# Three half feed-forwards of the second block by seven block products in place of eight, and a norm that squares tile by tile

## The chip, the cores and the metric

The kernel runs on one core of one Trainium2 chip, as one launch. The metric is the device time of that core in microseconds (us), the median over runs. The core has a matrix engine (TensorE, PE in the profile, with its weight loads as PEld), a vector engine (VectorE, DVE), a scalar engine (ScalarE, ACT), GpSimd (POOL) and SyncE (SP), which issues the weight transfers. Everything is float32. The runs of the kernel before: 3458.43, 3456.97 and 3460.97 us, median 3458.43.

## The reference

Two blocks of layers over 256 latent tokens with 1024 features; the second block also carries 256 context tokens. The change is in the second block, whose half feed-forward is:

```python
def swiglu(h, wg, wu, wd):
    return (jax.nn.silu(h @ wg) * (h @ wu)) @ wd

def half_ffn(h, g, shift, scale, gate, wg, wu, wd):
    return h + 0.5 * gate * swiglu(modulate(rms_norm(h, g), shift, scale), wg, wu, wd)

for l in range(DEPTH):          # DEPTH = 2; x: 256 latent tokens, ctx: 256 context tokens
    x   = half_ffn(x,   g_norm[l, 0], ml[0], ml[1], ml[2], ...)
    ctx = half_ffn(ctx, g_norm[l, 0], mc[0], mc[1], mc[2], ...)
    ... token mixing (attention, short convolution) on x and ctx ...
    x   = half_ffn(x,   g_norm[l, 2], ml[6], ml[7], ml[8], ...)
    if l < DEPTH - 1:
        ctx = half_ffn(ctx, g_norm[l, 2], mc[6], mc[7], mc[8], ...)
```

`wg` and `wu` are 1024 x 2816, `wd` is 2816 x 1024. `ml` and `mc` are modulation vectors of the latent and of the context tokens.

## The kernel before, in words

Activations are kept with features on the 128 partitions and tokens along the free axis. `x` is [128, 8 feature tiles, 512 tokens]: columns 0 to 255 are the context, 256 to 511 the latents. 2816 is 22 tiles of 128 (`FT`), 1024 is 8 (`KT`).

A half feed-forward (`HalfFfn`, run as half00, half01, half10 and half11, in that order, with the mixing stages mix0 behind half00 and mix1 behind half10) has three parts:

- the norm (`tensor_norm`, `scalar_norm`, `vector_norm`). ScalarE squares tiles 0, 2, 4, 6 (line 238) and VectorE tiles 1, 3, 5, 7 (line 224), each as its tile of `x` is ready; on VectorE the odd squares stand behind a wait for the last tile of `x` and the small scale operations (lines 1611, 1585). TensorE sums over partitions with a matrix of ones, eight matmuls in the order of the tiles, into `aux[0]`. ScalarE takes Ln and Exp (lines 241, 243) for the reciprocal root; VectorE scales (line 228) and ScalarE shifts (line 250), 16 half tiles each. The first group of matmuls behind it waits tile by tile, so it starts with the first shifted tile.
- the up part (`tensor_pairs`): 11 weight blocks of 2 MB, each with four groups (gate, up, gate, up) of 8 matmuls 128 x 128 by 128 x W. W is 512 in half00, half01 and half10, which carry context and latents, and 256 in half11. ScalarE takes Silu of the gate (line 1606), VectorE multiplies it with the up group into `big` (line 1618).
- the down part (`tensor_down`): 8 blocks of 1.4 MB, each with one group of 22 matmuls 128 x W. VectorE adds gate times result to `x` (line 1627).

PSUM has eight banks: `acc[0..3]` go round the groups, `aux[0..3]` serve the norms and the attention. A group waits until its bank was read (`acc_free`), and its last matmul raises `acc_full`. Weights go through four slots of 2 MB (`RING`, `SLOT`); SyncE issues block b once block b-4 is used up. `te.matmul` on float32 stands in the trace as two MATMUL records and two weight loads; all have line 130, since one helper (`mm`) issues them. The order on each engine is the order in which `tensor_program`, `scalar_program` and `vector_program` are written: each engine works its list in order and waits on semaphores. No planner changes it.

In the first block's recurrence (`scalar_scan`, `vector_scan`, four rounds) masks multiply 64 x 64 blocks, and one operand is copied with factor -1.

## Time and profile before

| | before |
|---|---|
| runs | 3458.43, 3456.97, 3460.97 us |
| profiled execution, its own time | 3464.32 us |
| span of the profile | 3463.0 us |
| mean granted TensorE clock | 0.986 |
| TensorE busy | 3323.2 us, 96% |
| VectorE busy | 751.0 us, 22% |
| ScalarE busy | 531.1 us, 15% |
| DMA, mean | 107 GB/s |
| half00, first matmul to last | 1236.9 to 1692.0 us |
| half01 | 2057.6 to 2514.0 us |
| half10 | 2525.4 to 2981.8 us |
| half11 | 3232.6 to 3461 us |

A start in the trace counts from the span's start. A row of the time order (timeline) gives start, length, engine, line, operation, output<-inputs, shapes and how many instructions were merged in it; in brackets the idle time of the engine before it and what ended it. The clock that a row of stretches (windows) gives is a share of full speed.

### The profile page before, as it was taken

Reading aid. Unit: us, or ns where it says so; the run is one execution under the profiler, and the core shown is the slowest. Engines: PE = TensorE matmul, PEld = TensorE weight load, DVE = VectorE, ACT = ScalarE, POOL = GpSimd, SP = SyncE. Lnnn points to the kernel's source line nnn. Section 1 sums busy time; section 2 is a strip of 40 time slices with the busy share of each in tenths; the row PEclk is TensorE's granted clock in tenths of the full one; section 3 lists DMA queues with packets and bytes.
Section 4 is the critical chain, followed back from the end, with each engine's and each line's share of the span. In section 5 each row is a group of like instructions: output and inputs, shape, how many; then the busy total and the mean of one; then the engine's idle time right before and its main releaser. Section 6 shows DMA issues by size and latency. Waiting matters only on the chain.

```text
span 3463.0 us, 33245 instructions
## 1 busy us (share of the span) xinstructions
PE 3323.2 (96%) x14466; PEld 2023.5 (58%) x14466; DVE 751.0 (22%) x1670; ACT 531.1 (15%) x1114; POOL 50.5 (1%) x78
## 2 busy tenths in 40 slices
PE   7889999998899999999999999999999999999999
PEld 5656678885688844444443644444444444555888
DVE  3255333123432110000115510000010000235100
ACT  1133222022221110000113310000010000223100
POOL 0000000020000000000001000000000000000000
PEclk9899999999999999999999999999999999999999
DMA  5359934463044522213203012222322222220343
GB/s 209 114 198 324 334 129 149 140 182 125 29 145 133 160 86 84 65 50 91 73 21 97 1 49 73 73 60 76 95 73 73 65 67 74 75 92 25 123 144 99
DMA packets 355813, 370.23 MB, mean 107 GB/s; under 512 B 7395, under 2 KB 282228, under 8 KB 355540
## 3 DMA queue, kind: packets, MB, share of 16 engines
q1 hardware_dynamic: 350224, 358.04, 32.6%
q0 software_dynamic: 2224, 5.38, 0.8%
q10 hardware_dynamic: 3220, 4.68, 0.4%
q8 instruction: 115, 1.88, 0.2%
q14 instruction: 30, 0.25, 0.0%
HBM read 367.03 MB, written 1.05 MB: 106 GB/s over the span
## 4 chain that ended last, share of the span: by engine, by line
PE 93%; DVE 4%; ACT 3%; issue 1%; DMA 0%; ACTq 0%; DVEq 0%
PE acc L130 82%; PE aux L130 10%; ACT sb_work L1486 0%; DVE sb_big L1333 0%; ACT sb_work L1350 0%; ACT sb_work L1352 0%; DVE sb_work L1538 0%; DVE sb_work L1554 0%; DVE sb_work L1535 0%; DVE sb_xn L228 0%; DMA sb_x<-xT 0%; DVE sb_work L1523 0%; ACT sb_rstd L241 0%; ACT sb_rstd L243 0%; ACT sb_xn L250 0%
## 5 line engine op out<-in xcount | busy, mean ns | idle before, releaser
L130 PE MATMUL acc<-sb_xn,weights 128*128 128x256 f32 (+1 forms) x5888 | 1842.9, 475 | 29.5 <-ACT sb_xn L250 17.1
L130 PEld LDWEIGHTS acc<-sb_xn,weights 128*128 128x128 f32 x5888 | 1120.4, 191 | 743.9 <-issue 645.0
L130 PE MATMUL acc<-sb_big,weights 128*128 128x256 f32 (+1 forms) x2304 | 727.0, 478 | 0.0
L130 PEld LDWEIGHTS acc<-sb_big,weights 128*128 128x128 f32 x2304 | 439.1, 191 | 286.2 <-issue 253.3
L1618 DVE TENSOR_TENSOR sb_big<-sb_work,acc 128x512 f32<-128x512 f32 (+1 forms) x88 | 54.6, 621 | 998.3 <-PE acc L130 998.3
L130 PE MATMUL aux<-sb_work 128*128 128x128 f32 (+8 forms) x1206 | 190.9, 340 | 35.5 <-DVE sb_work L1544 9.7
L1606 ACT ACTIVATE sb_work<-acc 128x512 f32<-128x512 f32 (+1 forms) x88 | 47.9, 544 | 973.1 <-PE acc L130 973.1
L130 PEld LDWEIGHTS aux<-sb_work 128*128 128x128 f32 (+4 forms) x1206 | 130.6, 180 | 113.7 <-issue 54.0
L1627 DVE SCALAR_TENSOR_TENSOR sb_x<-acc,sb_small,sb_x 128x256 f32<-128x256 f32 x56 | 24.9, 479 | 504.9 <-PE acc L130 504.9
L130 PE MATMUL acc<-sb_work,weights 128*128 128x256 f32 (+4 forms) x312 | 102.4, 467 | 6.1 <-DVE sb_work L1122 6.0
L238 ACT ACTIVATE sb_xn<-sb_x 128x256 f32<-128x256 f32 (+1 forms) x40 | 18.4, 496 | 471.4 <-DVE sb_x L1627 412.4
L130 PE MATMUL acc<-weights,sb_work 128*32 128x512 f32 (+1 forms) x608 | 88.9, 598 | 1.2 <-issue 1.2
L130 PE MATMUL aux<-sb_xn,sb_ones 128*128 128x256 f32 (+1 forms) x180 | 62.9, 496 | 23.6 <-ACT sb_xn L238 17.7
L1214 DVE SCALAR_TENSOR_TENSOR sb_work<-acc,sb_cols,sb_work 128x255 f32<-128x255 f32 x88 | 42.5, 482 | 195.0 <-ACT sb_work L1202 195.0
L130 PEld LDWEIGHTS acc<-sb_work,weights 128*128 128x128 f32 (+2 forms) x312 | 54.7, 179 | 46.4 <-issue 39.4
L1202 ACT ACTIVATE sb_work<-acc,sb_cols 128x256 f32<-128x256 f32 x88 | 49.7, 564 | 191.4 <-PE acc L130 191.4
L130 PEld LDWEIGHTS aux<-sb_xn,sb_ones 128*128 128x128 f32 x180 | 34.5, 199 | 49.0 <-issue 27.7
L130 PE MATMUL acc<-sb_big 64*128 64x512 f32 (+3 forms) x144 | 56.7, 528 | 1.8 <-DVE sb_work L1913 1.0
L272 DVE TENSOR_TENSOR sb_x<-acc,sb_x 128x256 f32<-128x256 f32 x32 | 13.6, 425 | 196.5 <-PE acc L130 196.5
L1359 POOL TENSOR_TENSOR sb_big<-sb_big,sb_rope 96x256 f32<-96x256 f32 (+1 forms) x32 | 23.2, 724 | 2174.0 <-PE aux L130 2174.0
L1851 ACT ACTIVATE sb_work<-acc,sb_work 128x512 f32<-128x512 f32 (+1 forms) x72 | 43.9, 614 | 43.4 <-DVE sb_work L1924 42.3
L1922 DVE TENSOR_REDUCE sb_work<-acc 128x1 f32<-128x512 f32 (+1 forms) x60 | 41.5, 691 | 28.9 <-PE acc L130 28.9
(260 smaller groups left out, 1583.2 us busy)
## 6 DMA issues: line engine op xcount, KB each, us to landing
weights<-ffn_w_up SPq DMA_DIRECT2D x88, 1024.0 KB, 7.9
weights<-w_mod SPq DMA_DIRECT2D x36, 2048.0 KB, 9.1
weights<-ffn_w_down SPq DMA_DIRECT2D x48, 1408.0 KB, 7.0
weights<-ffn_w_gate SPq DMA_DIRECT2D x44, 1024.0 KB, 5.5
weights<-w_in SPq DMA_DIRECT2D x8, 2048.0 KB, 8.1
weights<-mix_w_in SPq DMA_DIRECT2D x6, 2048.0 KB, 13.4
weights<-na_w_qkv SPq DMA_DIRECT2D x6, 2048.0 KB, 8.0
weights<-ple_w_gate SPq DMA_DIRECT2D x4, 2048.0 KB, 8.6
```

The lines of the kernel that those rows point to most:

```text
L130: return te.matmul(o, lhsT, rhs, start=start, stop=stop, skip_group_check=True)
L238: square_a.on(ac.activation(N.squares[:, k, :], x[:, k, N.t0:T2], ACT.Square))
L272: acc_free[g.bank].on(ve.tensor_tensor(x[:, k, t0:t1], acc[g.bank][:, 0:t1 - t0], x[:, k, t0:t1], ALU.add))
L1202: mid_tap.on(ac.activation(u, acc[g.bank][:, 0:L], ACT.Identity, scale=cols("ffn_cw", 1, 132 * F.i + 44 + t), bias=cols("ffn_cb", 1, 44 * ...
L1214: v_step.on(ve.scalar_tensor_tensor(u[:, 1:L], ps[:, 0:L - 1], cols("ffn_cw", 1, 132 * F.i + t), u[:, 1:L], ALU.mult, ALU.add))
L1359: hn_cos.on(gp.tensor_tensor(raw[:, CTX:], raw[:, CTX:], rot[1], ALU.mult))
L1606: acc_free[g.bank].on(ac.activation(F.sg[:, f % 2, :], acc[g.bank][:, 0:F.W], ACT.Silu))
L1618: acc_free[u.bank].on(ve.tensor_tensor(F.hid[:, f, :], F.sg[:, f % 2, :], acc[u.bank][:, 0:F.W], ALU.mult))
L1627: ve.scalar_tensor_tensor(x[:, k, a:e], acc[g.bank][:, a - t0:e - t0], gate_of(k, h), x[:, k, a:e], ALU.mult, ALU.add))
L1851: ins_ = ac.activation(mx_e[:, b, W * i:W * i + W], acc[b][:, W * i:W * i + W], ACT.Exp, bias=mx_st[:, 6 + 2 * b + i:7 + 2 * b + i], scale ...
L1922: v_step.on(ve.tensor_reduce(top, src, AX.X, ALU.max))
```

## The change

Two adjacent operands are treated as 2 x 2 blocks, and their product is made by the Strassen-Winograd scheme: seven block products in place of eight, with sums of blocks before and behind them.

Up part: block rows are gate and up weights of one 128-wide tile of the hidden dimension, the inner halves are feature tiles 0 to 3 and 4 to 7, and block columns are context and latents. So one step i (of 22) makes seven products of 4 matmuls 128 x 256, where two groups of 8 matmuls 128 x 512 stood. Down part: block rows are two neighbouring output tiles, the inner halves are hidden tiles 0 to 10 and 11 to 21; each of 4 steps makes seven products of 11 matmuls 128 x 256 in place of two groups of 22 matmuls 128 x 512. The order of the products is `PRODUCTS` = 1, 3, 2, 6, 7, 5, 4. Product 1 goes to bank A, is copied out by ScalarE, and product 2 is accumulated on it; products 7 and 4 share bank C in the same way, with VectorE reading in between.

VectorE makes the sums: four of the weights per step (`weight_sums`; 512 elements per partition in the up part, 1408 in the down part, one of them in place in the weight slot), four of the activations per part (`activation_sums`; 1024 and 2816 elements), and behind the products five sums of 256 elements that read PSUM. `weight_sums(0)` stands ahead of the norm on VectorE. Product 1 of step 0 waits for all tiles of the norm.

The norms of mix0, half10 and mix1 (`hooked`) are squared by ScalarE alone, two tiles behind each down step, into two buffers, and TensorE's eight matmuls of the norm stand in the down part of the feed-forward before (six behind product 2 of a step, two at its end). The norms of half00 and half01 keep the old form. half11 is unchanged.

In the recurrence of the first block a mask that held -upto and before holds upto and before for both uses, so that it is loaded once; the factor -1 moves from one copy of ScalarE to another and to one of VectorE. Some scratch areas have other addresses.

The diff, cut to its core:

```diff
+    def stream(loads=1):
+        return Block(b % RING, weights_in[b % RING].reserve(loads)(loads - 1), reuse, [])
...
     def tensor_norm(N):
-        W = T2 - N.t0
-        for k in range(KT):
-            te.wait_ge((square_a, square_v)[k % 2].sem, N.sq[1 - k % 2](k // 2))
-            ins_ = mm(aux[0][:, 0:W], ones[:], N.squares[:, k, :], k == 0, k == KT - 1)
-        sq_total.on(ins_)
+        for k in range(KT) if not N.hooked else ():
+            tensor_norm_tile(N, k)
+
+    def scalar_square(N, k):
+
+        ac.wait_ge(N.x_ready[k][0].sem, N.x_ready[k][1])
+        if k >= 2:
+            ac.wait_ge(sq_total.sem, N.total(k - 2))
+        square_a.on(ac.activation(N.squares[:, k % 2, :], x[:, k, N.t0:T2], ACT.Square))
...
-    sil, pick = area(work, 12128, KT, 32), area(work, 12384, 2)
-    side = area(work, 12400, 2, 128)
+    sil, pick = area(work, 12416, KT, 32), area(work, 12672, 2)
+    side = rope[:, 2, 384:512]
...
-        sc_tm.on(ac.activation(by_b, quads(aux[0][:]), ACT.Copy, scale=-1.0))
+        sc_tm.on(ac.copy(by_b, quads(aux[0][:])))
...
-        sc_uwa.on(ac.copy(uw[:, 4:8, :], quads(b1[:])))
+        sc_uwa.on(ac.activation(uw[:, 4:8, :], quads(b1[:]), ACT.Copy, scale=-1.0))
...
-        sc_uwv.on(ve.tensor_copy(uw[:, 0:4, :], quads(b0[:])))
+        sc_uwv.on(ve.tensor_scalar(uw[:, 0:4, :], quads(b0[:]), -1.0, None, ALU.mult))
...
+    PRODUCTS = (1, 3, 2, 6, 7, 5, 4)
+    hook_sq = area(xn, FH * L, 2, T2)
+    bank_a, bank_b, bank_c, bank_d, bank_e = acc[0], acc[1], acc[2], acc[3], aux[0]
...
+            self.norm = Norm(0, xv_w, lambda k, h: gsc[:, k, h:h + 1], x_ready, lambda k, h: mod[:, m0 + k, h:h + 1],
+                             extra, squares, hooked)
+            self.up = [stream(loads=2) for _ in range(FH)]
+            self.down = [stream() for _ in range(KT)]
+            self.last_up = last_done[-KT - 1]
...
+    def tensor_fast(F, following):
+        tensor_norm(F.norm)
+        for i in range(F.n):
...
+            for blk in F.blocks_of(i):
+                te.wait_ge(weights_in[blk.slot].sem, blk.arrived_at)
+            a11, a12, s3, a22 = F.weights(i)
+            s1, s2, s4 = F.sums(i)
+            t1, t2, t4 = sum_x if up else sum_h
+            src, kt = (xv_w, 4) if up else (hid, FH)
+            b11, t3, b21, b22 = src[:, 0:kt, 0:L], src[:, 0:kt, L:T2], src[:, kt:2 * kt, 0:L], src[:, kt:2 * kt, L:T2]
+            operands = {1: (a11, b11), 2: (a12, b21), 3: (s4, b22), 4: (a22, t4), 5: (s1, t1), 6: (s2, t2), 7: (s3, t3)}
+            banks = {1: bank_a, 2: bank_a, 3: bank_e, 4: bank_c, 5: bank_d, 6: bank_b, 7: bank_c}
+            for q in PRODUCTS:
+                if q == 1 and i and i <= FT:
+                    te.wait_ge(st_g1.sem, F.g1(i - 1))
+                elif q == 1 and i:
+                    te.wait_ge(st_x.sem, F.x(4 * (i - FT - 1)))
+                elif q == 3:
+                    te.wait_ge(st_s.sem, F.s(i))
+                    if i:
+                        te.wait_ge(st_c12.sem, F.c12(i - 1))
+                    if i == FT:
+                        te.wait_ge(st_hid.sem, F.hid(2 * FT - 1))
+                elif q == 2:
+                    te.wait_ge(st_u.sem, F.u(i))
+                elif q == 7 and i:
+                    te.wait_ge(st_c21.sem, F.c21(i - 1))
+                elif q == 4:
+                    te.wait_ge(st_v.sem, F.v(i))
+                if i in (0, FT) and q in (6, 7, 5, 4):
+                lhs, rhs = operands[q]
+                for k in range(kt):
+                    if i == 0 and q == 1 and k == 0:
+                        sig, value = F.norm.ready(KT - 1)
+                        te.wait_ge(sig.sem, value)
+                    if i == FT and q == 1:
+                        te.wait_ge(st_hid.sem, F.hid(2 * k + 1))
+                    ins_ = mm(banks[q][:, 0:L], lhs[:, k, :], rhs[:, k, :], k == 0 and q not in (2, 4), k == kt - 1)
+                F.done[i, q][0].on(ins_)
+                if q == 2 and i > FT:
+                    for k in (2 * (i - FT) - 2, 2 * (i - FT) - 1):
+                        tensor_norm_tile(following, k)
+        for k in (KT - 2, KT - 1):
+            tensor_norm_tile(following, k)
...
+        for i in range(F.n):
+            s = i % 2
+            ac.wait_ge(F.done[i, 1][0].sem, F.done[i, 1][1])
+            if i >= 2 and i - 2 < FT:
+                ac.wait_ge(st_hid.sem, F.hid(2 * (i - 2) + 1))
+            elif i >= 2:
+                ac.wait_ge(st_x.sem, F.x(4 * (i - 2 - FT) + 3))
+            st_u.on(ac.copy(pair_u[:, s, :], bank_a[:, 0:L]))
+            if i < FT:
+                ac.wait_ge(F.done[i, 2][0].sem, F.done[i, 2][1])
+                st_g1.on(ac.activation(pair_g1[:, s, :], bank_a[:, 0:L], ACT.Silu))
+                ac.wait_ge(st_c12.sem, F.c12(i))
+                st_g2.on(ac.activation(pair_g2[:, s, :], pair_g2[:, s, :], ACT.Silu))
+            elif i > FT:
+                scalar_square(following, 2 * (i - FT) - 2)
+                scalar_square(following, 2 * (i - FT) - 1)
+        scalar_square(following, KT - 2)
+        scalar_square(following, KT - 1)
+
+    def vector_fast(F):
+        hid = area(big, 0, FT, T2)
+        sig, value = F.norm.x_ready[KT - 1]
+
+        def weight_sums(i):
+            a11, a12, a21, a22 = F.weights(i)
+            s1, s2, s4 = F.sums(i)
+            for blk in F.blocks_of(i):
+                ve.wait_ge(weights_in[blk.slot].sem, blk.arrived_at)
+            if 2 <= i < FT:
+                ve.wait_ge(F.done[i - 2, 5][0].sem, F.done[i - 2, 5][1])
+            elif i > FT:
+                ve.wait_ge(F.done[i - 1, 5][0].sem, F.done[i - 1, 5][1])
+            v_step.on(ve.tensor_tensor(s1, a21, a22, ALU.add))
+            ve.wait_ge(v_step.sem, v_step.n)
+            v_step.on(ve.tensor_tensor(s2, s1, a11, ALU.subtract))
+            v_step.on(ve.tensor_tensor(a21, a11, a21, ALU.subtract))
+            ve.wait_ge(v_step.sem, v_step.n)
+            st_s.on(ve.tensor_tensor(s4, a12, s2, ALU.subtract))
...
+        def activation_sums(src, kt, t):
+            st_t.on(ve.tensor_tensor(t1, b12, b11, ALU.subtract))
+            ve.wait_ge(st_t.sem, st_t.n)
+            st_t.on(ve.tensor_tensor(t2, b22, t1, ALU.subtract))
+            st_t.on(ve.tensor_tensor(b12, b22, b12, ALU.subtract))
+            ve.wait_ge(st_t.sem, st_t.n)
+            st_t.on(ve.tensor_tensor(t4, b21, t2, ALU.subtract))
+
+        ve.wait_ge(sig.sem, value)
+        weight_sums(0)
+        v_step.on(ve.tensor_scalar(half_gate, mod[:, F.m0 + 16:F.m0 + 24, :], 0.5, None, ALU.mult))
+        vector_scales(F.l, 0 if F.j == 0 else 2, F.m0 + 8)
+        vector_norm(F.norm)
+        sig, value = F.norm.ready(KT - 1)
+        ve.wait_ge(sig.sem, value)
+        activation_sums(xv_w, 4, sum_x)
+        for i in range(F.n):
+            s, down = i % 2, i - FT
+            u, v, g1, g2 = (t[:, s, :] for t in (pair_u, pair_v, pair_g1, pair_g2))
+            if i < FT:
+                weight_sums(i + 1)
+            elif down == 0:
...
+            if down >= 0:
+                ve.wait_ge(F.done[i, 2][0].sem, F.done[i, 2][1])
+                add_back(2 * down, 0, bank_a[:, 0:L])
+            ve.wait_ge(st_u.sem, F.u(i))
+            ve.wait_ge(F.done[i, 6][0].sem, F.done[i, 6][1])
+            v_step.on(ve.tensor_tensor(u, u, bank_b[:, 0:L], ALU.add))
+            ve.wait_ge(v_step.sem, v_step.n)
+            ve.wait_ge(F.done[i, 7][0].sem, F.done[i, 7][1])
+            st_v.on(ve.tensor_tensor(v, u, bank_c[:, 0:L], ALU.add))
+            ve.wait_ge(F.done[i, 5][0].sem, F.done[i, 5][1])
+            v_step.on(ve.tensor_tensor(g2, u, bank_d[:, 0:L], ALU.add))
+            ve.wait_ge(st_v.sem, st_v.n)
+            v_step.on(ve.tensor_tensor(v, v, bank_d[:, 0:L], ALU.add))
+            ve.wait_ge(v_step.sem, v_step.n)
+            st_c12.on(ve.tensor_tensor(g2, g2, bank_e[:, 0:L], ALU.add))
+            if down >= 0:
+                ve.wait_ge(st_c12.sem, st_c12.n)
+                add_back(2 * down, 1, g2)
+                add_back(2 * down + 1, 1, v)
+                if i + 1 < F.n:
+                    weight_sums(i + 1)
+            ve.wait_ge(F.done[i, 4][0].sem, F.done[i, 4][1])
+            st_c21.on(ve.tensor_tensor(u, u, bank_c[:, 0:L], ALU.add))
+            ve.wait_ge(st_c21.sem, st_c21.n)
+            if i < FT:
+                ve.wait_ge(st_g2.sem, F.g2(i))
+                st_hid.on(ve.tensor_tensor(hid[:, i, L:T2], g2, v, ALU.mult))
+                ve.wait_ge(st_g1.sem, F.g1(i))
+                st_hid.on(ve.tensor_tensor(hid[:, i, 0:L], g1, u, ALU.mult))
+            else:
+                add_back(2 * down + 1, 0, u)
...
-    half00 = HalfFfn(0, 0, 0, ple1.x_ready, extra=(ctx_in, 32))
-    mix0 = Mixing(0, True, half00.x_ready)
-    half01 = HalfFfn(0, 1, 0, mix0.x_ready)
-    half10 = HalfFfn(1, 0, 0, half01.x_ready)
-    mix1 = Mixing(1, False, half10.x_ready)
+    half00 = FastFfn(0, 0, ple1.x_ready, extra=(ctx_in, 32))
+    mix0 = Mixing(0, True, half00.x_ready, hooked=True)
+    half01 = FastFfn(0, 1, mix0.x_ready, squares=area(big, 0, KT, T2))
+    half10 = FastFfn(1, 0, half01.x_ready, squares=hook_sq, hooked=True)
+    mix1 = Mixing(1, False, half10.x_ready, hooked=True)
```

## Rows read from the trace of the kernel before

**Rows 1.** The page, part 1 (busy time and share of span) and part 4 (chain that ended last).

```profile
PE 3323.2 (96%) x14466; PEld 2023.5 (58%) x14466; DVE 751.0 (22%) x1670; ACT 531.1 (15%) x1114; POOL 50.5 (1%) x78
...
PE 93%; DVE 4%; ACT 3%; issue 1%; DMA 0%; ACTq 0%; DVEq 0%
```

**Rows 2.** Time order, ScalarE: Silu of the gate in half00, steps 2 and 22.

```profile
1259.47 0.60 ACT L1606 ACTIVATE sb_work<-acc 128x512 f32<-128x512 f32 x1 [13.14 <-PE acc L130]
...
1534.14 0.60 ACT L1606 ACTIVATE sb_work<-acc 128x512 f32<-128x512 f32 x1 [13.14 <-PE acc L130]
```

**Rows 3.** Time order where matmuls are 128 x 256: ffn0's groups of 8, half11's of 22.

```profile
601.56 0.56 ACT L1202 ACTIVATE sb_work<-acc,sb_cols 128x256 f32<-128x256 f32 x1 [1.40 <-PE acc L130]
...
629.19 0.56 ACT L1202 ACTIVATE sb_work<-acc,sb_cols 128x256 f32<-128x256 f32 x1 [1.41 <-PE acc L130]
...
3394.29 0.48 DVE L1627 SCALAR_TENSOR_TENSOR sb_x<-acc,sb_small,sb_x 128x256 f32<-128x256 f32 x1 [9.08 <-PE acc L130]
...
3460.77 0.48 DVE L1627 SCALAR_TENSOR_TENSOR sb_x<-acc,sb_small,sb_x 128x256 f32<-128x256 f32 x1 [9.02 <-PE acc L130]
```

**Rows 4.** Stretch of ffn0: length, PE, PEld, DVE, ACT, POOL busy, clock, DMA.

```profile
600.00:640.00 40.00, 40.00 (x188) 35.20 (x187) 11.24 (x24) 6.90 (x14) 0.00 (x0) 1.00 0.42 110
```

**Rows 5.** Time order at the start of half00.

```profile
1226.02 0.42 DVE L1275 TENSOR_TENSOR sb_x<-sb_work,sb_x 128x256 f32<-128x256 f32 x1
...
1226.89 2.50 DVE L224 TENSOR_TENSOR sb_xn<-sb_x 128x512 f32<-128x512 f32 x4
...
1227.64 6.28 PE L130 MATMUL aux<-sb_xn,sb_ones 128*128 128x512 f32 x14 [0.42 <-DVE sb_xn L224]
...
1235.85 6.50 ACT L250 ACTIVATE sb_xn<-sb_xn,sb_mod 128x256 f32<-128x256 f32 x16 [0.55 <-DVE sb_xn L228]
1236.90 10.52 PE L130 MATMUL acc<-sb_xn,weights 128*128 128x512 f32 x20 [2.99 <-ACT sb_xn L250]
...
1245.74 0.60 ACT L1606 ACTIVATE sb_work<-acc 128x512 f32<-128x512 f32 x1 [2.09 <-PE acc L130]
```

**Rows 6.** Stretches at the same place: the granted clock.

```profile
1239.00:1241.00 2.00, 2.00 (x4) 0.89 (x3) 2.00 (x6) 2.00 (x6) 0.00 (x0) 0.50 0.00 0
1241.00:1243.00 2.00, 2.00 (x6) 0.79 (x5) 0.76 (x2) 1.98 (x5) 0.00 (x0) 0.99 0.00 0
```

**Rows 7.** Time order from half00 into mix0.

```profile
1673.19 0.88 DVE L1627 SCALAR_TENSOR_TENSOR sb_x<-acc,sb_small,sb_x 128x256 f32<-128x256 f32 x2 [18.01 <-PE acc L130]
1674.10 0.63 ACT L238 ACTIVATE sb_xn<-sb_x 128x512 f32<-128x512 f32 x1 [37.14 <-DVE sb_x L1627]
1674.75 1.28 ACT L239 ACT_TABLE_LOAD   x1
...
1692.08 0.88 DVE L1627 SCALAR_TENSOR_TENSOR sb_x<-acc,sb_small,sb_x 128x256 f32<-128x256 f32 x2 [18.01 <-PE acc L130]
...
1693.81 6.28 PE L130 MATMUL aux<-sb_xn,sb_ones 128*128 128x512 f32 x14 [0.92 <-DVE sb_xn L224]
1700.12 0.69 ACT L241 ACTIVATE sb_rstd<-aux,sb_small 128x512 f32<-128x512 f32 x1 [24.09 <-PE aux L130]
...
1703.08 9.25 PE L130 MATMUL acc<-sb_xn,weights 128*128 128x512 f32 x21 [2.99 <-ACT sb_xn L250]
```

**Rows 8.** Time order at the start of half01, TensorE and ScalarE.

```profile
2057.61 17.84 PE L130 MATMUL acc<-sb_xn,weights 128*128 128x512 f32 x34 [2.99 <-ACT sb_xn L250]
...
2067.76 0.60 ACT L1606 ACTIVATE sb_work<-acc 128x512 f32<-128x512 f32 x1 [3.40 <-PE acc L130]
```

**Rows 9.** Time order from half01 into half10, VectorE and TensorE.

```profile
2514.09 0.87 DVE L1627 SCALAR_TENSOR_TENSOR sb_x<-acc,sb_small,sb_x 128x256 f32<-128x256 f32 x2 [18.01 <-PE acc L130]
...
2525.43 5.46 PE L130 MATMUL acc<-sb_xn,weights 128*128 128x512 f32 x6 [2.99 <-ACT sb_xn L250]
```

**Rows 10.** Groups by line and shape: VectorE sums from SBUF, 1024 and 256 elements.

```profile
L474 DVE TENSOR_TENSOR sb_work<-sb_work 128x1024 f32<-128x1024 f32 x1 | 1.2, 1224 | 0.0
...
L1220 DVE TENSOR_TENSOR sb_big<-sb_work 128x256 f32<-128x256 f32 x44 | 18.7, 425 | 1.5
```

More of the change, by code:

```diff
@@ L2007, in tensor_program @@
         tensor_ple(ple1)
[L2008 removed]
+        tensor_fast(half00, mix0.norm)
         tensor_mixing(mix0)
[L2010 to L2011 removed]
+        tensor_fast(half01, half10.norm)
+        tensor_fast(half10, mix1.norm)
         tensor_mixing(mix1)
```

120 lines of the change are left out of this document (95 added, 25 removed).

## The prediction

> **What bounds the kernel now.** I read the page's busy times and its chain first, then the spacing of results in the two kinds of feed-forward, then the gaps between stages. TensorE is busy 96% of the span and carries 93% of the chain that ended last [rows 1]. So a half feed-forward is as long as its matmuls, plus the gap around its norm. The reader is to see how even the results come: from step 2 to step 22 of half00 the Silu starts 274.67 us apart over 20 steps, 13.73 us for 16 matmuls of 512 columns, or 0.8583 us each [rows 2]. The down part has the same pace: 18.89 us for 22 [rows 7]. Where a matmul has 256 columns, eight groups of 8 take 27.63 us in ffn0, 0.4317 us each, and seven groups of 22 take 66.48 us in half11, 0.4317 us each [rows 3]. Two things follow. A matmul of half the width costs 0.503 of the wide one, so the shorter products lose next to nothing. And a group of 8 has the same pace as a group of 22, so the change of bank and the waits that are already satisfied at a group's end cost some nanoseconds at most. ffn0 keeps that pace, with TensorE busy 40.00 of 40 us at full clock, while VectorE works 11.24 us of them [rows 4]. The rest of the time around a feed-forward is the norm: a gap of 11.0 us from half00's last matmul to mix0's first [rows 7].
>
> **The matmuls.** Before, each of the three feed-forwards has 44 x 8 + 8 x 22 = 528 matmuls of 0.8583 us, 453.2 us. After, it has 22 x 7 x 4 + 4 x 7 x 11 = 924 of 0.4317 us, 398.9 us. Saved: 54.3 us each, 162.9 us in all. A product is 4 or 11 matmuls long, shorter than any group in the rows. There are 26 x 7 = 182 handovers in each feed-forward, 546 in all. From groups of 8 and 22 I take them at nothing. If every one made TensorE really wait, the nearest row is a matmul that starts when a VectorE square ends: the first square takes some 0.69 us from 1226.89 and the matmul starts at 1227.64, 0.06 us later [rows 5]. That gives 33 us as the upper bound. I take 1 us, as the rows with satisfied waits are the nearest: **161.9 us saved**.
>
> **Does anything reach TensorE late inside a step?** Up part: a product is 4 x 0.4317 = 1.73 us, a step 12.09 us. Product 2 waits for ScalarE's copy of product 1 (256 elements; the Silu of 512 takes 0.60 us [rows 2]), and product 3 stands in between with 1.73 us. Even a table load of 1.28 us [rows 7] before that copy would end within 0.2 us of that. VectorE has per step four weight sums of 512 elements (the four squares of 512 took 2.50 us [rows 5]; two waits for its own results add some 0.1 us each, 2.7 us) and eight sums of 256 at 0.48 us or less [rows 3], so some 6.7 of 12.09 us. The tightest point is product 6: behind product 4 of the step before, VectorE has three of the small sums (1.5 us), then the weight sums, until 4.2 us; product 6 ends at 4 x 1.73 = 6.9 us. Nothing waits.
>
> Down part: a step is 33.2 us. The weight sums of the next step share one buffer, so they stand between the end of product 5 and the start of the next product 3: products 4 and 1, 22 x 0.4317 = 9.50 us. In this window VectorE has five operations of 256 (5 x 0.51 = 2.55 us) and four sums of 1408 elements. No row has that size; 256 elements take 0.425 and 1024 take 1.224 us [rows 10], so 1.04 ns per element more, 1.62 us at 1408, and with two of the four overlapping slightly 6.5 us. Together 9.05 us: a slack of only 0.45 us. I take no stall. Each 0.1 us by which a sum is longer costs nothing up to the slack and then 0.4 us at each of 9 places. The activation sums of the down part (2816 elements, 3.1 us each) begin some 1.5 us into products 1, 3, 2 (14.2 us); product 6 needs only two of them, 7.7 us. The loads keep four slots and the same 2 MB per 24.2 us in place of 27.5; the DMA share in ffn0, which takes 2 MB in 13.8 us, is 0.42 [rows 3, 4].
>
> For a sum of 1408 elements the Trainium skill (VectorE: DVE Perf Modes, The TRN2 errata) gives (N + 151) / 0.96 ns, which would be 1.62 us as an estimate. No run here shows this size yet; the sum would be the same.
>
> **The entries of half00 and half01** get longer in two ways. First, `weight_sums(0)` stands on VectorE ahead of the odd squares, and behind it queue the scales and the squares, for which TensorE waits: 2.7 us. Nothing covers it. Second, product 1 waits for the last shifted tile. Before, the first matmul started at 1236.90, 1.05 us behind the first shift, and the last shift ended at 1235.85 + 6.50 = 1242.35 [rows 5]; the matmuls in between ran beside the norm. After, the start moves 5.45 us later. Together 8.15 us each, **16.3 us lost**. What the slow clock costs I leave as it is: half00's first group took 8.84 us in place of 6.87 [rows 5], with a clock of 0.50 of full speed (1.2 GHz) after a gap of 2.99 us, and full speed from 1241 on [rows 6]; half01's took 10.15 us [rows 8]. These starts already pay 2.0 and 3.3 us, and a longer gap can hardly make them pay much more.
>
> **The hooked norms** (mix0, half10, mix1). Six of their eight matmuls of 512 now stand among the products: 6 x 0.858 = 5.15 us each, **15.4 us lost**; the seventh runs while VectorE adds the last tile. The gap shrinks. After the last product: two operations of VectorE 1.05, square 0.63 [rows 7], table load 1.28 (longer than the last norm matmul, 0.86), then, as before, from Ln to the first matmul 1703.08 - 1700.12 = 2.96 us [rows 7], with handovers 6.0 us. Before it was 1703.08 - 1692.08 = 11.0 us. So mix0 and mix1 gain 5.0 us each, **10 us won**, and with their six matmuls come out even. half10 gains the same 5.0, but its product 1 waits 5.45 us more for the last shift. The result is 11.4 us against 2525.43 - 2514.09 = 11.34 [rows 9]: nothing. `weight_sums(0)` is covered there: it ends at 1.05 + 2.7 = 3.75 us, and the reciprocal root is set at 4.4; without that cover it would cost 2.7 us.
>
> The Trainium skill (TensorE: Matmul & The Clock Gate, HAM oscillation) has a rule that speaks against this change: gaps in which TensorE idles throw it back to half clock, and each longer gap at an entry (8.5 us here) risks a restart at half speed. The trace agrees that such a gap can do it; as all three starts are already slow in places, the sum would be up to 3 us worse for each by it.
>
> **The rest.** In the recurrence, one mask load becomes smaller and a factor moves between copies of the same size in four rounds. half11 and the first block's norms get an extra signal per matmul. No row separates these; I take 0, bounds -1 to +1 us.
>
> **Sum.** 161.9 - 16.3 - 15.4 + 10 - 0 = 140.2 us. On the profiled execution 3464.3 - 140.2 = 3324.1; the runs' median lies 5.9 us below that execution, so **3318 us**.
>
> **Rivals.** (a) Handovers cost: each product waits some 0.06 us for something, 546 x 0.06 = 33 us, 3351. For it: twice to three times as many waits per matmul as in any group shown, and products of 1.73 us. Against: groups of 8 and 22 at one pace. (b) The slack of 0.45 us in the down part isn't there, because sums of 1408 elements read weight slots beside transfers and weight loads and take, say, twice as long: 4 x 1.62 - 0.45 = 6.0 us late at 9 places, 54 us, 3372. In the up part the doubled sums would end at 6.9 us, just in time. For it: no row has such a sum. Against: VectorE's 28% beside TensorE in ffn0 shows no slowing. (c) Slower than before: the clock. If short waits between products, not only gaps at the norm, make it fall to 1.2 GHz, a feed-forward takes up to twice its 398.9 us. The gain of 140 us is gone once 280 of the 1197 us of matmuls run at half clock, and at 350 us the kernel stands at 3493. Against: the small gaps between groups in ffn0 leave the clock at 1.00 [rows 4]. (d) The change doesn't do what it says, in that the norm in the down part isn't even: if the gap at mix0, half10 and mix1 stays at 11 us because another wait is last, 15 us, 3333.
>
> **Chances.** Forecast 0.70 (own range 3306 to 3326: clock at the starts -6 to +6, handovers, recurrence), (d) 0.08, (a) 0.11, (b) 0.08, (c) 0.03. The range takes in the forecast, (d) and half of (a): 3305 to 3343. A measurement of this kernel tells 0.2%, some 7 us, from no change. Only (c) lies there or beyond: faster 0.97, same 0.01, slower 0.02.
>
> **What would show it.** Right: product spacing of 1.73 us, up steps of 12.09, down steps of 33.2 plus 1.72 where two norm matmuls stand; TensorE idle only at the entries, 8.5 us from the last norm matmul to product 1; 6 us from half00's last product to mix0's first matmul. Wrong: a group of idle times of TensorE ahead of product 3 released by VectorE's weight sums (b), idle time or a pace above 0.432 us spread over all products (a), a granted clock below 1.00 inside the steps (c).

## The result, and the profile after

The changed kernel takes 3326.43 us (median; 3324.26 to 3327.29) against 3459.02 us of the kernel before in the same comparison: ratio 0.9616, 95% interval 0.9599 to 0.9632. That is 132.6 us less. The prediction was 3318 us, 140.2 us of gain in the profiled execution. The profiled executions stand 138.5 us apart (3464.32 and 3325.86). So the sum of the prediction is 1.7 us off, with an error of 4.5 us inside it that other differences partly cancel, and most of the 8 us by which the median misses comes from elsewhere. The median lies inside the range of 3305 to 3343 us, and just above the narrower one of 3306 to 3326 that the forecast gave for itself. One later execution of the changed kernel took 4228.42 us at a mean granted clock of 0.744, unlike all others; its cause is open, and it is left out of every median here.

The page of the kernel after, parts 1 and 4 (to be read against [rows 1]):

```profile
PE 3161.3 (95%) x16842; PEld 2474.9 (74%) x16842; DVE 1237.0 (37%) x2528; ACT 579.4 (17%) x1270; POOL 50.3 (2%) x78
...
PE 91%; DVE 4%; ACT 3%; issue 1%; DMA 1%; ACTq 0%; DVEq 0%
```

TensorE works 161.9 us less, VectorE 486 us more, and the kernel is still bound by TensorE. VectorE's share of the chain stays at 4%, in spite of its 486 us of new work. The stretch of half00's up part shows why (columns: length, then busy time of PE, PEld, DVE, ACT, POOL, granted clock, DMA share, GB/s):

```profile
1260.00:1500.00 240.00, 240.00 (x1114) 211.27 (x1113) 114.52 (x237) 23.09 (x60) 0.00 (x0) 1.00 0.26 80
```

TensorE never idles in 240 us and VectorE is busy 114.52 of them. The copy of each product 1 (time order of the kernel after, ScalarE: start, length, what; in brackets the idle time before) has a period of 12.09 us, seven products of 1.73 us, all through the up part of each of the three feed-forwards:

```profile
1261.86 0.37 ACT L1776 COPY sb_work<-acc 128x256 f32<-128x256 f32 x1 [1.80 <-PE acc L130]
...
1273.94 0.37 ACT L1776 COPY sb_work<-acc 128x256 f32<-128x256 f32 x1 [1.80 <-PE acc L130]
...
1286.03 0.37 ACT L1776 COPY sb_work<-acc 128x256 f32<-128x256 f32 x1 [1.79 <-PE acc L130]
```

In the down part, around the tightest place, time order of VectorE and TensorE:

```profile
1544.48 1.62 DVE L1801 TENSOR_TENSOR sb_work<-weights 128x1408 f32<-128x1408 f32 x1
...
1549.33 1.62 DVE L1806 TENSOR_TENSOR sb_work<-weights,sb_work 128x1408 f32<-128x1408 f32 x1
...
1551.74 4.91 PE L130 MATMUL aux<-sb_big,sb_work 128*128 128x256 f32 x22
```

A sum of 1408 elements takes 1.62 us, as estimated, beside transfers that move 290 GB/s from 1544 to 1552 us. The last one ends at 1550.95 and product 3, which reads it, starts at 1551.74 without idle time: a slack of 0.79 us where 0.45 us was predicted.

The entry of half00 is where the prediction was off ([rows 5] before). Time order of the kernel after:

```profile
1225.26 0.69 DVE L1801 TENSOR_TENSOR sb_work<-weights 128x512 f32<-128x512 f32 x1
...
1228.34 2.50 DVE L237 TENSOR_TENSOR sb_xn<-sb_x 128x512 f32<-128x512 f32 x4
...
1229.09 7.97 PE L130 MATMUL aux<-sb_xn,sb_ones 128*128 128x512 f32 x14 [3.08 <-DVE sb_xn L237]
...
1239.00 6.49 ACT L263 ACTIVATE sb_xn<-sb_xn,sb_mod 128x256 f32<-128x256 f32 x16 [0.55 <-DVE sb_xn L241]
...
1245.63 3.75 PE L130 MATMUL acc<-sb_xn,weights 128*128 128x256 f32 x8 [8.58 <-ACT sb_xn L263]
1249.18 2.28 PE L130 MATMUL aux<-sb_xn,sb_work 128*128 128x256 f32 x8
1251.30 1.89 PE L130 MATMUL acc<-sb_xn,weights 128*128 128x256 f32 x8
1253.02 1.89 PE L130 MATMUL acc<-sb_work 128*128 128x256 f32 x8
```

The weight sums hold the squares back (idle time 3.08 us in place of 0.42), and product 1 waits for the last shift (8.58 in place of 2.99). The third thing was not in the sum: the seven norm matmuls take 7.97 us in place of 6.28. The granted clock of the kernel after (same columns as above) shows it at half speed there:

```profile
1229.00:1233.00 4.00, 3.92 (x5) 1.63 (x6) 1.84 (x4) 0.00 (x0) 0.00 (x0) 0.57 0.68 216
1233.00:1237.00 4.00, 4.00 (x10) 1.52 (x8) 0.00 (x0) 0.00 (x0) 0.00 (x0) 1.00 0.00 0
```

In the first 4 us TensorE runs at a mean clock of 0.57, mostly at 1.2 GHz, and starts 5 of the trace's matmul records, against 10 in the next 4 us at 2.4 GHz. At the start of half01 it is the same, with 3.91 us of idle time (1.26 before) and 8.85 us:

```profile
2005.17 2.50 DVE L237 TENSOR_TENSOR sb_big<-sb_x 128x512 f32<-128x512 f32 x4
2005.92 8.85 PE L130 MATMUL aux<-sb_big,sb_ones 128*128 128x512 f32 x14 [3.91 <-DVE sb_big L237]
...
2023.34 3.75 PE L130 MATMUL acc<-sb_xn,weights 128*128 128x256 f32 x8 [8.57 <-ACT sb_xn L263]
```

From half00 into mix0, where the hooked norm was to pay ([rows 7] before; last product to first matmul 11.0 us), time order of the kernel after:

```profile
1652.05 0.42 DVE L1861 TENSOR_TENSOR sb_work<-sb_work,acc 128x256 f32<-128x256 f32 x1 [2.62 <-PE acc L130]
...
1653.03 0.63 ACT L279 ACTIVATE sb_xn<-sb_x 128x512 f32<-128x512 f32 x1 [3.33 <-DVE sb_x L1837]
1653.68 1.28 ACT L252 ACT_TABLE_LOAD   x1
...
1657.99 10.43 PE L130 MATMUL acc<-sb_xn,weights 128*128 128x512 f32 x18 [3.16 <-ACT sb_xn L263]
```

From 1652.01 (the last product's end, just ahead of L1861) to 1657.99 there are 5.98 us: 6.0 were predicted.

### The profile page after: what moved, and what is told of

Same layout as the page of the kernel before. It is cut to its first block, busy times and chain, and to the rows that moved or that the text cites. A ratio compares the mean times of both kernels' runs of the same rounds, so it can differ in the third digit from the quotient of the medians.

```text
span 3324.6 us, 39320 instructions
## 1 busy us (share of the span) xinstructions
PE 3161.3 (95%) x16842; PEld 2474.9 (74%) x16842; DVE 1237.0 (37%) x2528; ACT 579.4 (17%) x1270; POOL 50.3 (2%) x78
## 4 chain that ended last, share of the span: by engine, by line
PE 91%; DVE 4%; ACT 3%; issue 1%; DMA 1%; ACTq 0%; DVEq 0%
PE acc L130 75%; PE aux L130 16%; ACT sb_xn L263 1%; ACT sb_work L1508 0%; DVE sb_big L1355 0%; ACT sb_work L1372 0%; DMA weights<-mix_w_in 0%; ACT sb_work L1374 0%; DVE sb_work L1560 0%; DVE sb_work L1576 0%; DVE sb_work L1557 0%; DMA sb_x<-xT 0%; DVE sb_work L1545 0%; ACT sb_rstd L254 0%; ACT sb_rstd L256 0%
## 5 line engine op out<-in xcount | busy, mean ns | idle before, releaser
L130 PE MATMUL acc<-sb_xn,weights 128*128 128x256 f32 (+1 forms) x5360 | 1310.5, 400 | 47.7 <-ACT sb_xn L263 34.4
L130 PEld LDWEIGHTS acc<-sb_xn,weights 128*128 128x128 f32 x5360 | 1020.6, 191 | 298.3 <-issue 161.0
L130 PE MATMUL acc<-sb_big,weights 128*128 128x256 f32 x2040 | 448.3, 379 | 0.0
L130 PE MATMUL acc<-sb_work 128*128 128x256 f32 x1320 | 308.4, 379 | 0.0
L130 PE MATMUL acc<-sb_work,weights 128*128 128x256 f32 (+4 forms) x1104 | 285.7, 404 | 6.1 <-DVE sb_work L1144 6.0
L130 PEld LDWEIGHTS acc<-sb_work 128*128 128x128 f32 x1320 | 250.8, 190 | 37.9 <-issue 4.3
L130 PEld LDWEIGHTS acc<-sb_work,weights 128*128 128x128 f32 (+2 forms) x1104 | 205.1, 187 | 66.9 <-issue 39.4
L1844 DVE TENSOR_TENSOR sb_work<-sb_work,acc 128x256 f32<-128x256 f32 x78 | 32.9, 421 | 259.2 <-PE acc L130 259.2
L130 PE MATMUL aux<-sb_xn,sb_work 128*128 128x256 f32 x528 | 125.8, 381 | 0.0
L130 PEld LDWEIGHTS aux<-sb_xn,sb_work 128*128 128x128 f32 x528 | 101.4, 192 | 14.2
L1847 DVE TENSOR_TENSOR sb_work<-sb_work,acc 128x256 f32<-128x256 f32 x78 | 32.9, 422 | 137.1 <-PE acc L130 137.1
L1849 DVE TENSOR_TENSOR sb_work<-sb_work,acc 128x256 f32<-128x256 f32 x78 | 32.9, 421 | 131.9 <-PE acc L130 131.9
```

The lines of the kernel that those rows point to most:

```text
L130: return te.matmul(o, lhsT, rhs, start=start, stop=stop, skip_group_check=True)
L1844: v_step.on(ve.tensor_tensor(u, u, bank_b[:, 0:L], ALU.add))
L1847: st_v.on(ve.tensor_tensor(v, u, bank_c[:, 0:L], ALU.add))
L1849: v_step.on(ve.tensor_tensor(g2, u, bank_d[:, 0:L], ALU.add))
```

## The experiments

"Entry" below is the time from the end of the last addition to x to the first matmul of product 1. What a stage "takes" is counted from its first matmul to the end of its last addition to x, so a stage and the entry of the next one together make the whole. All ratios are against the kernel before, all diffs against the kernel after. Where a run is said to be some us less than after, it is against 3326.43 us.

**The kernel after once more**, so that the later runs have a neighbour.

> The changed kernel once more, beside the next three on the same chip. Both theories: 3326 us, and entries of half00 and half01 of 20 to 22 us from the last tile of x to product 1, of which the clock at half speed takes a part that differs by some us from run to run.

3324.7 us, ratio 0.9612 (0.9599 to 0.9625); with these four executions the median of all eight of the kernel after is still 3326.43. Entries 20.4, 21.3 and 10.6 us, as in the first profile. What is read from the entries repeats to 0.1 us.

**The weight sums behind the squares.** VectorE squares first, then prepares step 0.

```diff
+        if behind_squares is not None:
+            behind_squares()
         ve.wait_ge(rstd_set.sem, N.rstd)
...
-        weight_sums(0)
...
-        vector_norm(F.norm)
+        vector_norm(F.norm, lambda: weight_sums(0))
```

> The first weight sums move from ahead of the norm's odd squares to behind them on VectorE, nothing else. My theory: in half00 and half01 the sums (2.7 us) stretched TensorE's idle time before the second norm matmul to 3 to 4 us, and the norm matmuls behind it then ran at half clock for a while (7.97 and 8.85 us where seven took 6.28 before). With the sums away both go: 2.7 us twice, and 1.7 and 2.6 us of slow clock, 9.7 us in all, 3317 us; the seven norm matmuls take 6.3 us again. Rival: they were slow because of the weight transfers that run at that moment; then only 5.4 us are won, 3321 us, and they still take 8 to 9 us.

3323.12 us, 0.9610 (0.9596 to 0.9623). Time order of this kernel, TensorE, at both entries:

```profile
1229.32 6.28 PE L130 MATMUL aux<-sb_xn,sb_ones 128*128 128x512 f32 x14 [0.42 <-DVE sb_xn L237]
...
2002.78 6.28 PE L130 MATMUL aux<-sb_big,sb_ones 128*128 128x512 f32 x14 [1.26 <-DVE sb_big L237]
```

Without the long idle time the seven matmuls are back at 6.28 us. The entries fall by 4.4 and 5.2 us to 16.0 each, 9.6 us in all (theory: 9.7, of which only 5.4 are the sums themselves). Over all runs it is the same: in the six profiled kernels and repeats that leave the sums in front and the gap empty the seven take 7.8 to 8.0 us in half00 and 7.7 to 8.9 in half01, and in the six whose idle time there is 0.4 and 1.3 us they take 6.28 each time. A transfer into the weights runs beside these matmuls in both kernels, here even a denser one, at full clock:

```profile
1229.32:1233.00 3.68, 3.68 (x9) 1.77 (x10) 3.65 (x6) 1.26 (x1) 0.00 (x0) 1.00 1.09 371
```

So the transfer isn't what slowed them. But the median fell by only 3 us, to near the rival's 3321 and not for its reason: mix1 took 238.1 us in place of 234.4, half10 1.4 us more and half11 1.7.

**The same again**, since that remainder was unexplained.

> The weight sums behind the squares once more. In its first profile the entries of half00 and half01 got 4.3 and 5.2 us shorter, 9.5 in all, but the median only 4 us (3323 against 3327), because the mixing stage mix1 and half11 took 5.3 us longer than in the changed kernel, with a slow clock inside mix1. Theory: that is chance (where the slow clock falls in the attention of mix1), and a second set of runs lies anywhere from 3316 to 3324 us, with the entries again 9.5 us shorter. Rival: the earlier start itself costs the time later, so that the median stays at 3323 us and mix1 and half11 are longer again by 5 us.

3322.66 us, 0.9608 (0.9595 to 0.9621). Entries 16.0 us each again, and mix1 238.1 and half11 230.4 again: the numbers are those of the rival, not of the theory of chance. Where mix1's time goes is one stretch of its attention. Twenty microseconds of it in this kernel, and the same place in the kernel before:

```profile
2984.30:3004.30 20.00, 20.00 (x75) 11.10 (x75) 8.93 (x26) 6.80 (x16) 0.00 (x0) 0.77 0.06 19
```

```profile
3132.80:3152.80 20.00, 20.00 (x96) 11.90 (x95) 11.59 (x32) 8.28 (x20) 0.00 (x0) 1.00 0.08 24
```

TensorE counts as busy all through in both, but at a clock of 0.77 the trace holds 75 matmul records in place of 96. Ahead of it, in both kernels, stands a stretch in which TensorE is busy 15.38 of 20 us (2964.3 to 2984.3 and 3112.8 to 3132.8).

**The kernel before once more**, to see whether an unchanged kernel does this too.

> The kernel before once more. Its profiled execution took 3464.3 us against 3459 for the median of its runs. If that distance is chance (how much of the entries falls on half clock), this profile lies at 3457 to 3462 us; if profiling makes this kernel longer by 5 us, it lies at 3464 again.

3460.18 us, 0.9997 (0.9988 to 1.0005), but its profiled execution took 3472.54 us, outside both expectations. Its mix1 took 237.8 us in place of 233.4, with the same dip:

```profile
3135.00:3155.00 20.00, 20.00 (x76) 11.11 (x76) 9.02 (x26) 6.79 (x16) 0.00 (x0) 0.78 0.05 15
```

Its first block took 4.7 us more, half11 1.7 more, half10 3 less. half10's start shows that the same wait goes either way: 2.99 us of idle time behind the same matmuls, and then, in the first profile and in this one (granted clock 0.51 and 1.00, 8 and 14 matmul records):

```profile
2525.43:2531.43 6.00, 6.00 (x8) 2.51 (x9) 4.85 (x13) 5.98 (x15) 0.00 (x0) 0.51 0.01 3
```

```profile
2530.48:2536.48 6.00, 6.00 (x14) 2.73 (x15) 4.86 (x13) 5.98 (x15) 0.00 (x0) 1.00 0.01 3
```

So one execution of one kernel may or may not fall to half clock in these places, at 3 to 5 us each. A profile alone can't be trusted to better than that. The dip (mix1 at 237.8 to 238.8 us) is there in this run, in both kernels with the sums moved, with tile by tile, with both edits and with eight products, and absent (234.4 to 234.6) in the other seven profiles of the changed kernel and its variants. So no single edit decides it. Nor does the stage's time alone: mix1 starts at 2844.27 us in the repeat with the sums moved and dips, and at 2844.39 in the kernel with filled gaps and doesn't. The kernel after and the one with the sums moved each showed the same state in both of their profiles, the kernel before showed both states; what sets it stays open.

**Product by product, tile by tile.** Products 1, 3 and 2 of step 0 wait for each shifted tile as they read it.

```diff
-                    if i == 0 and q == 1 and k == 0:
-                        sig, value = F.norm.ready(KT - 1)
+                    if i == 0 and q in (1, 3, 2):
+                        sig, value = F.norm.ready(k if q == 1 else kt + k)
```

> Products 1, 3 and 2 of step 0 wait for the norm tile by tile, as the first group did in the kernel before; nothing else. My theory: product 1 starts some 5.4 us earlier, products 1 and 3 run beside the shifts, and product 6 starts 3.0 us earlier at full clock, up to 5.0 us where the slow clock after the gap now falls into time that waits for tiles anyway: 9 to 15 us over three entries, 3311 to 3317 us. Rival: the slow clock only moves with the start, so that nothing beyond 1 to 2 us each is won: 3320 to 3323 us.

3316.83 us, 0.9589 (0.9576 to 0.9602): 10 us less than after. The entries are 14.7, 15.8 and 5.0, each 5.5 to 5.7 us shorter. The feed-forwards take 408.7 us each in place of 407.4, 407.6 and 406.7, since some of the wait is now between the products. The second term of the entries was a real wait, and most of it can be had back (12 of 17 us).

**Both edits.**

> Both edits: weight sums behind the squares, and step 0 tile by tile. My theory: the two add up, 3326 - 9.7 - 12 = 3304 us (3300 to 3309). Rival: they take from the same slow clock, and together give no more than the larger of the two, 3314 us.

3308.32 us, 0.9564 (0.9551 to 0.9577), 18 us less than after: entries 10.5, 10.5 and 4.9. In the entries the gains of the two edits add up (9.9 us in half00, from 4.4 and 5.7); the median is 4 us above the theory, and mix1 takes 238.8 us here. Time order of this kernel, TensorE, at half00:

```profile
1224.35 6.28 PE L130 MATMUL aux<-sb_xn,sb_ones 128*128 128x512 f32 x14 [0.42 <-DVE sb_xn L237]
1233.61 3.60 PE L130 MATMUL acc<-sb_xn,weights 128*128 128x256 f32 x8 [2.99 <-ACT sb_xn L265]
```

**The norm at the end.** The eight squares and norm matmuls stand behind the last product in place of between the products.

```diff
-                if q == 2 and i > FT:
-                    for k in (2 * (i - FT) - 2, 2 * (i - FT) - 1):
-                        tensor_norm_tile(following, k)
-        for k in (KT - 2, KT - 1):
+        for k in range(KT):
             tensor_norm_tile(following, k)
```

(ScalarE's squares likewise.)

> The squares and the eight norm matmuls of mix0, half10 and mix1 all stand at the end of the feed-forward before, as one piece, with the same two buffers; the products are unchanged. My theory (interleaving moves 5.15 us into the steps and takes as much off the gap): the steps get 5.15 us shorter, the gap from the last product to the next stage's first matmul grows from 6.0 to some 10 us, so 3326 - 15.4 + 12.6 = 3323 us, 3320 to 3327. Rival: interleaving was a real gain, the norm's matmuls among the products cost nothing there; then 12 to 15 us slower, 3338 to 3341 us.

3324.92 us, 0.9607 (0.9592 to 0.9623). Time order of this kernel, TensorE, from half00 into mix0:

```profile
1642.91 4.91 PE L130 MATMUL acc<-sb_work,weights 128*128 128x256 f32 x22
1647.66 7.60 PE L130 MATMUL aux<-sb_xn,sb_ones 128*128 128x512 f32 x16
1658.41 7.11 PE L130 MATMUL acc<-sb_xn,weights 128*128 128x512 f32 x16 [3.15 <-ACT sb_xn L263]
```

The feed-forwards take 402.3, 402.4 and 401.7 us in place of 407.4, 407.6 and 406.7 (5.0 to 5.2 less each; six matmuls of 0.858 are 5.15), and the entries behind them are 9.6, 15.5 and 9.9 us in place of 5.0, 10.6 and 5.0 (4.6 to 4.9 more). The norm among the products is even, as the sum had it: the matmuls cost TensorE nearly the same in either place. Besides, mix0 takes 341.6 us here in place of 344.1: its first 8 us run at a granted clock of 1.00, against 0.57 in the kernel after. Whether the eight matmuls right ahead of the gap do that, or chance, one profile doesn't tell.

**Eight products.** Product 5 is computed twice, so that TensorE has eight block products and all else stays. The result isn't changed by it.

```diff
+                if q == 5:
+                    for k in range(kt):
+                        ins_ = mm(banks[q][:, 0:L], lhs[:, k, :], rhs[:, k, :], k == 0, k == kt - 1)
```

> Product 5 is computed twice, so that each step has eight products of the same size in place of seven. My theory (TensorE's matmuls alone set the pace, 0.4317 us each, and handovers cost nothing): 132 matmuls more in each of three feed-forwards, 57.0 us each, 171 us, 3497 us, 1.1% slower than the kernel before. Rival (VectorE or the handovers have a share in the pace of a step): part of the eighth product is hidden, 3440 to 3480 us.

3503.33 us, 1.0116 (1.0098 to 1.0134): 44 us slower than before, with all of the additions and none of the saving. The feed-forwards take 464.4, 464.0 and 464.0 us, 57.1, 56.4 and 57.2 more, where 132 matmuls of 0.4317 us make 57.0. The steps are one product longer to the hundredth:

```profile
1264.18 0.37 ACT L1779 COPY sb_work<-acc 128x256 f32<-128x256 f32 x1 [1.80 <-PE acc L130]
...
1277.99 0.37 ACT L1779 COPY sb_work<-acc 128x256 f32<-128x256 f32 x1 [1.80 <-PE acc L130]
```

13.81 us are 8 x 1.727. Only the number of matmuls sets the pace. The 6 us by which the median lies above the theory of 3497 are in mix0 and mix1, which took 3.4 and 3.6 us more than after; the added products don't explain that, and a dip of the clock as above would.

**One sum more in the down part.** One weight sum of 1408 elements is made twice with the same result.

```diff
             v_step.on(ve.tensor_tensor(s2, s1, a11, ALU.subtract))
+            if i > FT:
+                ve.wait_ge(v_step.sem, v_step.n)
+                v_step.on(ve.tensor_tensor(s2, s1, a11, ALU.subtract))
```

> In the down part one of the four weight sums of 1408 elements is made twice in the last three of four steps. My theory: in the trace of the changed kernel the sums end 0.79 us before product 3 starts, and one sum more costs 1.65 us, so product 3 waits 0.86 us in 9 steps: 7.7 us, 3334 us, and TensorE shows 9 idle times of 0.9 us ahead of product 3. Rival: VectorE has more room than that, because product 3 waits for something else: no change, 3326 us.

3336.38 us, 0.9638 (0.9623 to 0.9653). What TensorE waits for in this kernel between 1500 and 1660 us (us in total, times, longest):

```profile
PE aux L130 <- DVE sb_work L1809: 2.3, 3, 0.8
```

The same view of the kernel after, from 1240 to 1640 us, holds no wait of a product for VectorE, only the entry:

```profile
PE acc L130 <- ACT sb_xn L263: 8.6, 1, 8.6
```

1.65 us more of VectorE make TensorE idle for 0.8 us, so there is a slack of some 0.8 us, three times in each feed-forward. They get 3.2 to 3.3 us longer, which is more than 3 x 0.8. From one product's start to the next the trace shows the rest: product 3 starts 5.68 us behind product 1 in place of 4.75, and the product behind it 4.85 us later in place of 4.74. That is 1.03 us per step; in an unbroken row product 3 starts at 1551.74, before the record of the product ahead of it ends (1551.90), and behind a wait it doesn't.

**The idle gaps filled.** TensorE runs matmuls of 256 columns, which nobody reads, while it would wait: 6 behind the first norm matmul, 18 ahead of product 1.

```diff
+    def busy(n):
+        for _ in range(n):
+            mm(aux[2][:, 0:L], ones[:], rope[:, 0, 0:L])
...
+            if k == 0:
+                busy(fill)
...
+        tensor_norm(F.norm, 6)
+        busy(18)
```

> The changed kernel, with matmuls that nobody reads (128 x 256, into a bank that is free here) in TensorE's idle time at the three entries: 6 behind the first norm matmul in half00 and half01, 18 between the norm and product 1 in all three. They end before what TensorE waits for. Theory (the slow clock is a consequence of the idle gap, and has a price of its own): the seven norm matmuls take 6.3 us again (were 7.97 and 8.85) and products 1, 3 and 2 take 5.2 us (were 7.4, 7.65 and 6.8): 4.3 + 6.3 = 10.5 us won although work was added, 3317 us. Rival (the slow time is not the idle gap's doing): no change or slower, 3326 us or more.

3313.99 us, 0.9583 (0.9570 to 0.9596): 12 us less than after with more work. Time order of this kernel, TensorE, at half00:

```profile
1226.97 2.75 PE L130 MATMUL aux<-sb_rope,sb_ones 128*128 128x256 f32 x12
1230.14 6.28 PE L130 MATMUL aux<-sb_xn,sb_ones 128*128 128x512 f32 x14 [0.42 <-DVE sb_xn L237]
1236.26 7.93 PE L130 MATMUL aux<-sb_rope,sb_ones 128*128 128x256 f32 x36
1244.99 1.97 PE L130 MATMUL acc<-sb_xn,weights 128*128 128x256 f32 x8 [0.80 <-ACT sb_xn L263]
...
1250.25 1.89 PE L130 MATMUL acc<-sb_work 128*128 128x256 f32 x8
...
1644.33 4.91 PE L130 MATMUL acc<-sb_work,weights 128*128 128x256 f32 x22
```

The stretch of half00, granted clock 1.00 from the first product to the last:

```profile
1245.00:1649.00 404.00, 404.00 (x1860) 353.42 (x1861) 182.72 (x322) 32.36 (x78) 0.00 (x0) 1.00 0.27 78
```

The weight sums are still ahead of the squares, and the norm matmuls take 6.28 us all the same; product 1 takes 1.8 us in place of 3.55. So it is the idle time, not the work beside it, that made them slow. The entries are 18.7 us (20.4 and 21.3), and each feed-forward takes 405.2 us, 1.5 to 2.4 less. From product 1's first matmul to the last product's end there are 404.25 us in each of the three, where the bare count and six norm matmuls give 398.9 + 5.15 = 404.05: at full clock the 182 handovers of a feed-forward cost 0.2 us at most.

**The best version.** Both edits, and all eight squares of half00's and half01's norms on ScalarE, so that VectorE has only the weight sums there.

```diff
-        for k in range(1, KT, 2) if not N.hooked else ():
+        for k in range(1, KT, 2) if not (N.hooked or N.alone) else ():
...
-        for k in range(0, KT, 2) if not N.hooked else ():
+        for k in range(0, KT, 1 if N.alone else 2) if not N.hooked else ():
```

> Both edits (weight sums behind, step 0 tile by tile), and in half00 and half01 all eight squares on ScalarE, so that TensorE does not wait for VectorE between norm matmul 1 and 2. Theory: Ln starts 1.0 us earlier in half00 and 1.5 us in half01; 3308 - 2.5 = 3306 us. Rival: ScalarE's squares become the pace in half00, where all eight stand behind the last sigmoid: nothing gained there, 3307 us.

3299.79 us (3296.95 to 3304.64), 0.9543 (0.9530 to 0.9556): 159 us faster than before and 27 us faster than after. Norm matmuls run without a gap in between (time order, TensorE):

```profile
1220.89 7.13 PE L130 MATMUL aux<-sb_xn,sb_ones 128*128 128x512 f32 x16 [0.99 <-ACT sb_xn L254]
...
1986.97 7.03 PE L130 MATMUL aux<-sb_big,sb_ones 128*128 128x512 f32 x16
```

Entries are 9.8 and 8.9 us, 2.2 us less than with the two edits alone, where 2.5 were expected. The median fell by 8.5: mix1 at 234.5 (238.8) and half11 at 228.7 (230.4) are 6.1 us of it, the dip that comes and goes.

**The same with filled gaps.** To the best version, six unread matmuls ahead of product 1.

> The same with 6 idle-time matmuls between the norm and product 1 at the three entries. Theory: with the start tile by tile the slow clock falls into time in which TensorE waits for tiles, so that little is left to win: 0 to 3 us, 3303 to 3306 us. Rival: the slow clock still costs as much as in the changed kernel, then some 6 us: 3300 us.

3302.09 us, 0.9556 (0.9543 to 0.9569), no gain, although the clock was full. Time order of TensorE at half00's product 1 and product 2 in the best version, and below it with the filled gap:

```profile
1231.02 3.63 PE L130 MATMUL acc<-sb_xn,weights 128*128 128x256 f32 x8 [2.99 <-ACT sb_xn L266]
...
1237.05 1.89 PE L130 MATMUL acc<-sb_xn,weights 128*128 128x256 f32 x8
```

```profile
1233.89 3.00 PE L130 MATMUL acc<-sb_xn,weights 128*128 128x256 f32 x8 [0.40 <-ACT sb_xn L266]
...
1239.92 1.89 PE L130 MATMUL acc<-sb_xn,weights 128*128 128x256 f32 x8
```

Product 2 starts 6.03 us behind product 1 in both. Where product 1 starts with its first tile and then waits for the next ones, half clock in its first microseconds falls into waiting time.

Entries of half00, half01 and half10, and the medians, us:

| kernel | half00 | half01 | half10 | median |
|---|---|---|---|---|
| before | 10.5 | 10.5 | 10.5 | 3459.0 |
| after | 20.4 | 21.3 | 10.6 | 3326.4 |
| weight sums behind the squares | 16.0 | 16.0 | 10.5 | 3323.1 |
| tile by tile | 14.7 | 15.8 | 5.0 | 3316.8 |
| both | 10.5 | 10.5 | 4.9 | 3308.3 |
| gaps filled | 18.7 | 18.7 | 10.6 | 3314.0 |
| best | 9.8 | 8.9 | 4.9 | 3299.8 |

## Why the prediction was right, point by point

**What bounds the kernel, and the matmuls (161.9 us saved): right.** From the first product's matmul to the last one's end, the three feed-forwards take 406.38, 406.64 and 405.76 us in place of 455.13, 456.44 and 456.35, so 149.14 us less. The norm matmuls among the products account for 15.45 us. The slower starts are 1.83 us cheaper than before. After, product 6 starts 7.39, 7.65 and 6.77 us behind product 1, against 5.26 in the kernel with filled gaps, 6.0 us in all. Before, the first four wide matmuls took 5.21, 6.52 and 6.42 us in place of 3.43, 7.9 us in all. 149.14 + 15.45 - 1.83 = 162.8 us, against the 162.9 of the bare count. So the 546 handovers cost nothing that can be seen; rival (a) falls, and the 1 us taken for them was too much. The up steps stand 12.09 us apart and the down steps 33.24, and 34.95 with two norm matmuls, as forecast. The eight-product kernel shows the same from the other side, and the one with filled gaps bounds the handovers at 0.2 us per feed-forward.

**Nothing late inside a step: right, with the tight place where it was said to be.** The weight sum takes 1.62 us and the slack is 0.79 us. The Trainium skill (VectorE: DVE Perf Modes, The TRN2 errata) gave 1.62 us for this size, and the trace agrees. Rival (b) falls; the kernel with one sum more shows the price if the slack goes, 1.03 us of the step for 1.65 us of VectorE.

**The entries (16.3 us lost): this step failed, by 4.5 us.** Measured is 9.94 and 10.8 us, 20.8 in all. The two named parts are right: the weight sums 2.66 and 2.65 us (predicted 2.7), the wait for the last shift 5.59 and 5.58 (predicted 5.45). What failed is the sentence that a longer gap "can hardly make them pay much more". It looked only at the matmuls behind the long gap, which were slow already; those inside the norm ran at full clock before and pay 1.69 and 2.57 us now. The weight sums put an idle time of 3.08 and 3.91 us ahead of them. Behind the long gap the cost did stay level: 6.0 us in place of 7.9. The rule of the Trainium skill (TensorE: Matmul & The Clock Gate, HAM oscillation) that idle gaps throw TensorE back to half clock was the one to price here. The trace agrees with it, and its place was the short gap, not the long one. The kernels with the sums moved and with the gaps filled both bring 6.28 us back, by different means.

**The hooked norms (15.4 lost, 10 won, half10 even): right.** The gaps at mix0 and mix1 are 5.98 us each, from 11.0. half10's entry, counted from the last matmul before it, is 11.56 us in place of 11.38. Rival (d) falls. With the norm at the end the kernel takes the same time within its scatter (3324.92 us), so this part of the change is even, as the terms said.

**The clock inside the steps (rival c): right that it doesn't fall.** It is 1.00 over 240 us with a product boundary every 1.73 us. The rival's price was twice too low, though: a matmul at half clock costs its own time once more (0.85 us from one record to the next in half00's slow norm matmuls, 0.43 in the fast ones), so 140 of the 1197 us at half clock would have used up the gain, not 280.

**The rest (0, within 1 us).** The first block is 1.2 us faster and mix1 with half11 1.1 us slower. The kernels compared with themselves differ by more than that in these places, so nothing is put down to the edits of the recurrence.

**The sum.** 162.8 + 1.8 - 15.4 - 20.8 + 10.1 - 0.2 + 0.1 = 138.4 us, against 138.5 between the profiles and 140.2 predicted. The 4.5 us too little at the entries are partly cancelled by the cheaper starts (1.8) and the matmuls (0.9), which is luck. **The other 6.5 us of the miss come from the last line.** It subtracted 5.9 us because before's profiled execution lay that far above its median, and took it that after's would too; after's lies 0.6 us below its median (3325.86 and 3326.43). The second profile of the kernel before, 3472.54 us, shows that such a distance belongs to one execution, not to the program.

## What to carry to other kernels

Where TensorE is the bound and the operands sit in SBUF, seven products for eight brought nearly the full eighth of the matmul time here (54.3 of 453.2 us, 12.0%), so long as VectorE's sums end before the product that reads them; count that slack at the tightest place. Put preparation for the first step behind the squares on the engine that makes both, and let the first products wait tile by tile: here that is worth a further 18 us. Price an idle time not only by its length but by what TensorE runs next, and take the expected median from medians, not from one profile.
